# Two fused transformer blocks on one core: modulation sums and filling blocks placed anew in the written-out order

## The reference, cut to what matters

```python
D_MODEL = 1024; SEQ = 256; DEPTH = 4            # two tiles of 128 tokens
def first_block(x, c, ...):
    cond = jax.nn.silu(c)
    for i in range(DEPTH):                      # kinds: gla, sgu, fox, gla
        mod = (cond @ w_mod[i] + b_mod[i])[:, None, :]      # 1024 x 3072 weights per layer
        shift, scale, gate = jnp.split(mod, 3, axis=-1)
        h = rms_norm(x, norm_pre_g[i]) * (1.0 + scale) + shift
        o = (gla_mixer, sgu_mixer, fox_mixer)[i % 3](h, ...)
        x = x + gate * rms_norm(o, norm_post_g[i])
    return x
def second_block(x, ...):
    h = x
    h = h + hybrid_mixer(rms_norm_2(h, norm_mix), ...)      # convolution and dilated attention
    h = h + peer_ffn(rms_norm_2(h, norm_ffn), ...)
    return rms_norm_2(h, final_norm)
def peer_ffn(u, w_query, sub_keys, expert_down, expert_up):
    q = xf @ w_query                            # 8 heads, two halves of 128
    s = einsum(q, sub_keys)                     # 128 scores a half
    ...                                         # top 16 of each half, top 16 of their sums: idx, gates
    a = gelu(einsum('cd,ced->ce', xc, expert_down[ic]))     # 128 rows of 1024 floats a token
    return einsum('ce,ced->cd', gc * a, expert_up[ic])
```

## Time and profile before

| | |
|---|---|
| median of three executions | 1745.24 us (1738.43 to 1745.35) |
| profiled execution, device time | 1739.41 us |
| its span in the trace | 1737.6 us |
| busy: PE, DVE, ACT, POOL | 80%, 60%, 25%, 28% of the span |
| moved by DMA | 591.53 MB, 340 GB/s over the span |
| chain that ended last | DVE 8%, DMA 8%, issue 3%, PE 1% of the span |

### The profile page before, as it was taken

The page is one execution under the profiler, slowest core; times in us unless marked ns, Lnnn a source line. Parts: engine busy times, 40 slices in busy tenths (PEclk is TensorE's granted clock), DMA queues, the critical chain, the costliest instruction groups (busy, mean ns, idle before and its releaser), DMA issues. The chain is left out here.

```text
span 1737.6 us, 13867 instructions
## 1 busy us (share of the span) xinstructions
PE 1393.7 (80%) x4158; PEld 717.6 (41%) x4158; DVE 1047.5 (60%) x2197; ACT 433.1 (25%) x974; POOL 490.7 (28%) x498
## 2 busy tenths in 40 slices
PE   6998988978999999999777777699787647666665
PEld 6454435444444455444354343455333312222222
DVE  3645554553233222313797998788866778877876
ACT  1221413423423421102133232132002221111111
POOL 2101210210000000000445546355344545444441
PEclk9998998989999999999897888798888878898898
DMA  9978884978556776887999989999999999999995
GB/s 386 377 256 303 312 340 171 347 282 295 213 207 219 277 265 242 290 293 265 402 361 357 413 339 403 412 400 413 410 414 414 348 412 422 421 422 421 422 421 248
DMA packets 108941, 591.53 MB, mean 340 GB/s; under 512 B 12450, under 2 KB 12706, under 8 KB 60612
## 3 DMA queue, kind: packets, MB, share of 16 engines
q0 software_dynamic: 67776, 312.56, 45.4%
q1 hardware_dynamic: 41092, 278.10, 42.2%
HBM read 589.55 MB, written 1.05 MB: 340 GB/s over the span
## 5 line engine op out<-in xcount | busy, mean ns | idle before, releaser
L948 PE MATMUL bank<-ring,hT 128*128 128x512 f32 x1888 | 866.6, 615 | 39.6 <-DVE room L1920 12.1
L948 PEld LDWEIGHTS bank<-ring,hT 128*128 128x128 f32 x1888 | 366.5, 198 | 482.2 <-issue 449.8
L877 POOL DMA_INDIRECT room<-in_peer_down,idx x92 | 102.5, 1114 | 525.1 <-DVE idx L1781 401.8
L1798 DVE CUSTOM_DVE_ANT_0 room<-room 128x1024 f32<-128x1024 f32 x180 | 218.6, 1221 | 50.6 <-DMA room<-in_pair,idx 38.4
L1203 PE MATMUL bank<-room 128*128 128x512 f32 x284 | 150.9, 676 | 96.5 <-ACT room L1493 94.2
L1813 DVE SCALAR_TENSOR_TENSOR x<-room,pcoef,x 128x1024 f32<-128x1024 f32 x121 | 155.7, 1287 | 28.0 <-DMA room<-in_peer_up,idx 27.5
L877 POOL DMA_INDIRECT room<-in_peer_up,idx x104 | 114.0, 1096 | 88.6 <-DVE pa L1798 42.3
L1203 PEld LDWEIGHTS bank<-room 128*128 128x128 f32 x284 | 57.5, 215 | 190.8 <-issue 97.2
L849 POOL DMA_DIRECT2D room<-in_w_mod x80 | 42.2, 528 | 326.3 <-DVE room L1567 206.5
L877 POOL DMA_INDIRECT room<-in_pair,idx x88 | 97.0, 1102 | 108.5 <-PE bank L1203 50.6
L927 PE MATMUL bank<-cst,room 128*128 128x128 f32 x424 | 64.7, 297 | 55.3 <-ACT room L1439 24.1
(11 more groups left out here) (304 smaller groups left out, 1527.4 us busy)
## 6 DMA issues: line engine op xcount, KB each, us to landing
ring<-in_wpk SPq DMA_DIRECT2D x248, 1024.0 KB, 7.0
room<-in_w_mod POOLq DMA_DIRECT2D x80, 512.0 KB, 8.2
room<-in_w_mod SPq DMA_DIRECT2D x8, 1024.0 KB, 15.8
room<-in_norm_post_g POOLq DMA_DIRECT2D x4, 512.0 KB, 5.0
rowb<-in_gate_bias SPq DMA_DIRECT2D x4, 512.0 KB, 9.0
room<-in_peer_up,idx POOLq DMA_INDIRECT x104, 12.5
room<-in_peer_down,idx POOLq DMA_INDIRECT x92, 12.4
room<-in_pair,idx POOLq DMA_INDIRECT x88, 14.3
```

The lines of the kernel that those rows point to most:

```text
L877: return pool.indirect_dma_start(out=dst, out_offset=None, in_=A[table][0] if table != "pair" else A[table], in_offset=bass.IndirectOffset ...
L948: last = mm(bank[p][:, :], lhs, ring[:, h % 4, k * N:(k + 1) * N], start=(kk == 0), stop=(h == halves[-1] and k == 3))
L1798: v.tensor_tensor_reduce(out=row, in0=row, in1=u_(g // MINE), scale=1.0, scalar=0.0, op0=ALU.mult, op1=ALU.add, accum_out=pa[:, g // TOPK ...
```

## The change

Six edits, all in what order the same work is issued, but for the first:

1. `PE_PIECES` goes from six pieces to two. Pieces 9, 11, 13 and 15 are summed on DVE, and PE's 32 matmuls for them are gone.
2. A block's pieces are now put behind its `ev` and the steps that follow it, ahead of the next block, instead of straight behind its `mm`. How many a block gets comes from `PIECES_AT`.
3. Gaps: one of the two behind `out2` is moved to between `in2` 3 and `in2` 4 of tile 0.
4. The gap ahead of `merged_T` is gone, so `(1, in2, 0)` comes behind `ho` and `(1, in2, 1)` behind the first ticks.
5. For tile 0 each of the first score steps and `choose` comes one query block sooner.
6. At the end the last four picks make two groups of two, their additions are pulled into ticks 272 to 275, and the last four ticks are gone.

```diff
 def out_chunks(t, L):
-            "gap twice"]
+            "gap" if L == 2 else "gap twice"]
 def fox_chunks(t, L):
             b(3, [], [("unit", t, 1), ("forget_sum", t)]),
+            "gap",
             b(4, [], [("quad_T", t, 0), ("quad_S", t, 0)]),
 def hyb_chunks(t):
             b(0, name="attn"), b(1, name="attn"), b(0, name="conv"), b(1, name="conv"),
-            "gap",
             b(0, name="ho", pre=[("merged_T", t)]), b(1, [("ffn_norm", t)], name="ho"),
             "gap",
-            b(0, name="query", pre=[("norm_in", t, 5)]),
-            b(1, [("score_T", t, 0)], name="query"),
-            b(2, [("score_S", t, 0), ("score_T", t, 1)], name="query"),
+            b(0, [] if t else [("score_T", t, 0)], name="query", pre=[("norm_in", t, 5)]),
+            b(1, [("score_T", t, 0)] if t else [("score_S", t, 0)], name="query"),
+            b(2, ([("score_S", t, 0)] if t else []) + [("score_T", t, 1)], name="query"),
...
-PE_PIECES = (5, 7, 9, 11, 13, 15)
+PE_PIECES = (5, 7)
-TICKS = PICKS + REST + LEAD[1]
+TICKS = PICKS + REST + 2
...
-    return u < 7 * TOPK or u % 4 == 3 or (u % 2 and (u < MINE or u >= PICKS - 8))
+    return u < 7 * TOPK or (u % 4 == 3 and u < PICKS - 4) or (u % 2 and u < MINE) \
+        or u >= PICKS - 2 or (u % 2 and PICKS - 8 <= u < PICKS - 4)
...
 def added_at(v):
+    if v >= PICKS - 8:
+        return tick_of(PICKS - 2) + (v - PICKS + 8) // 2
     return tick_of(v) + LEAD[v // MINE]
...
-GROUPS = [(hh * TOPK, TOPK) for hh in range(PH)] + [(MINE + 4 * m, 4) for m in range(MINE // 4)]
+GROUPS = [(hh * TOPK, TOPK) for hh in range(PH)] + [(MINE + 4 * m, 4) for m in range(MINE // 4 - 1)] \
+    + [(PICKS - 4, 2), (PICKS - 2, 2)]
...
-    if mm[2] == "in0":
-        return (4, 4, 3, 2, 2, 2)[mm[3]]
-    return 4 + mm[3] if mm[2] == "out0" else 3
+PIECES_AT = {"in0": (4, 4, 4, 3, 3, 2), "out0": (4, 2), "in1": (4, 4, 4, 4, 3, 3), "out1": (3, 3),
+             "in2": (3, 3, 3, 3, 2, 2, 2, 2), "out2": (4, 2)}
...
         order += pre
         if mm:
             order.append(mm)
-        for _ in range(pieces_at(mm)):
-            if piece < len(PIECES):
-                order.append(("mod", piece))
-                piece += 1
...
         order += post
         if mm:
+            for _ in range(PIECES_AT[name][n] if name in PIECES_AT else 0):
+                order.append(("mod", piece))
+                piece += 1
             order += pending
             pending = []
-            if name == "query" and n == 2:
+            if name == "query" and n == 1:
                 order.append(("choose", 0))
```

More of the change, by code:

```diff
@@ L272 @@
 DVE_NTH = {u: i for i, u in enumerate(ON_DVE)}
-ADDS = {added_at(v): [v] for v in range(PICKS)}
+ADDS = {k: [v for v in range(PICKS) if added_at(v) == k] for k in range(TICKS)}
 def adds_of(k):
-    return ADDS.get(k, [])
+    return ADDS[k]
 def sums_at(hh):
@@ L289 @@
 EXP_AT = {sums_at(hh): hh for hh in range(T * PH) if hh != PH - 1}
-GROUPS = [(hh * TOPK, TOPK) for hh in range(PH)] + [(MINE + 4 * m, 4) for m in range(MINE // 4)]
+GROUPS = [(hh * TOPK, TOPK) for hh in range(PH)] + [(MINE + 4 * m, 4) for m in range(MINE // 4 - 1)] \
+    + [(PICKS - 4, 2), (PICKS - 2, 2)]
 GROUP_AT = {tick_of(g + n - 1) + 1: i for i, (g, n) in enumerate(GROUPS)}
 def group_of(v):
-    return v // TOPK if v < MINE else PH + (v - MINE) // 4
+    return next(i for i, (g, n) in enumerate(GROUPS) if g <= v < g + n)
 WAY = {"norm_in": 110, "low": 10, "decay": 12, "qk_T": 15, "level": 25, "cross": 30, "heads": 80, "gated_T": 50,
@@ L346, in tick @@
         self.at += 1
-def pieces_at(mm):
-    if mm is None:
-        return 0
-    if mm[2] == "in0":
-        return (4, 4, 3, 2, 2, 2)[mm[3]]
-    return 4 + mm[3] if mm[2] == "out0" else 3
+PIECES_AT = {"in0": (4, 4, 4, 3, 3, 2), "out0": (4, 2), "in1": (4, 4, 4, 4, 3, 3), "out1": (3, 3),
+             "in2": (3, 3, 3, 3, 2, 2, 2, 2), "out2": (4, 2)}
 def make_order():
@@ L397, in make_order @@
                 order.append(("sines", 0))
+            for _ in range(PIECES_AT[name][n] if name in PIECES_AT else 0):
+                order.append(("mod", piece))
+                piece += 1
             order += pending
             pending = []
-            if name == "query" and n == 2:
+            if name == "query" and n == 1:
                 order.append(("choose", 0))
-                rows.tick()
-            if name == "query" and n == 3:
-                rows.tick()
-                rows.tick()
+            if name == "query" and n >= 2:
+                for _ in range(n - 1):
+                    rows.tick()
     order += pending
@@ L992, in _ @@
             pe.wait_ge(S("cond"), 1)
-            for piece in PE_PIECES[:2]:
+            for piece in PE_PIECES:
                 piece_columns(piece, use("mod_cols", 0)[1])
@@ L1002, in _ @@
                         pe.wait_ge(S(f"ev{p}"), n // 2)
-                    if L == 0:
-                        for piece in PE_PIECES[2:]:
-                            piece_columns(piece, p)
                     pe.wait_ge(S(f"sums_init{L % 2}"), sums_set(L))
```

## The result

The changed kernel takes 1753.41 us in the median of 8 runs (1750.9 to 1758.21), the kernel before 1745.3 us (8 runs, 1738.43 to 1752.99). The ratio is 1.0055, with a 95% interval from 1.0039 to 1.0071: slower, by 8 us. The forecast was 1745, no change that can be told (0.48), with 0.30 for slower; the time lies in the range given (1731 to 1759), the direction was not the one forecast. The profiled execution has a span of 1751.3 us, 13.7 longer than the one of before, which was some 6 us under its median.

What follows compares the result with a forecast made beforehand. Before the first gather (821.25 us) PE's work and its waits for DVE bound the kernel, behind it DMA bytes. Terms: -8.5 + 4.5 - 2 + 1.3 = -4.7, so 1739.4 becomes 1744, as a median 1745 us; range 1731 to 1759.

Steps and rivals of the forecast that it cites:

- Start: Up to level 1 of tile 0: +7 us at `low`, of which +3 (between 0 and +7) stays at level 1.
- `out0`: Tile 0's `out0`: shorter wait for `post1` (0.8 us) and 16 matmuls in 7.1 us, +6, account +9.
- `in1`: Up to layer 1's gates: three more pieces on a full DMA, partly regained by +1.5; account from +9 to +6.
- the third rival: DMA-bound already in `in1`: DVE falls behind at both gates, later pieces take 12.4 us to land; 1754 to 1760 us (0.20).
- The second gate: Layer 1's second gate: tile 1's levels 3 and 4 come 13.7 us later, plus 1.9 for the clock; account -9.5.
- the gate's wait is short: Rival: transfers behind layer 1's second gate land in 5.3 us; 1729 to 1735 us (0.22).
- `out1`: Pieces 64 to 66 ahead of tile 1's levels 5 to 7: PE's wait of 3.01 us grows by 3.9; account -13.
- `in2` and the attention: Filling block covers two waits in `in2`, +5 (+2 to +7); fewer late pieces in attention, +3 wait, +2 clock; account -3.
- `out2`: Tile 1's `center` delays DVE's copy for `out2` 0: -5 wait, -2 clock, +1.5 at `post1`, together -5.5; account -8.5.
- First choice, give-back, tail: First gather 12.4 us sooner, 7.9 given back to weight loads (+4.5), -2 for DVE's elementwise work, +1.3 at the end.
- first choice sooner gives nothing: Rival: DVE sets the pace from 885 us on and uses up the 12.4 us; 1750 to 1755 us (0.08).
- two signs of being wrong: DVE's wait behind layer 1's second gate under 5 us, or the first gather before 812 us.

Runs made afterwards that it cites:

- changed_pieces_back: The changed kernel with the modulation pieces back where they stood, in the old counts; all other edits stay: 1737.8 us, 0.996 of the kernel before.
- pieces_moved: The kernel before with only the modulation pieces moved behind evacuations and steps, six pieces still on PE: 1766.2 us, 1.0134.
- two_pieces_on_pe: The kernel before with only two modulation pieces summed on PE, the other pieces where they stood: 1740.69 us, 0.9981.
- levels_first: The changed kernel with the sums of pieces 61 to 63 behind tile 1's levels 3 and 4 on DVE: 1742.76 us, 0.9992 of the kernel before.
- post_row_later: The changed kernel with POOL fetching the next post-norm row behind piece 63, no longer ahead of pieces 61 to 63: 1746.24 us, 1.0017 of the kernel before.
- filler_moved: The kernel before with one filling block moved from behind `out2` to between `in2` 3 and 4: 1747.49 us, 1.0024.
- choice_sooner: The kernel before with no filling block ahead of `merged_T` and the first choice behind query 1: 1736.04 us, 0.9963.
- three_edits_out0: The kernel before with two pieces on PE, first choice sooner, new tail, and `out0`'s pieces behind `post0` and `post1`: 1727.48 us, 0.9908.
- best_combination: The kernel before with two pieces on PE, sooner choice, new tail, `out0`'s pieces behind `post0` and `post1`, post-norm row fetched later: 1720.89 us, 0.9874.

## Why the prediction was wrong

**The step that failed is "Start", "I put +3 there, between 0 and +7".** It measured -2.2. I had seen that the places of pieces 24 to 27 come free some 5 us later, and they did (they were fetched from 65.83 us on, before from 60.01). But I took these 5 us off the +7 won at `low`, as if level 1 came behind `low`. It does not: it waits for the sum of the last piece ahead of it. Piece 27 was summed 6.5 us later than before, one piece fewer stood ahead of level 1 (piece 28 had been summed 4.25 us behind piece 27), and the difference is the -2.2. Of the 6.2 us won at `low` nothing arrives: PE's wait for level 1 grew from 2.49 to 10.88 us. The kernel changed_pieces_back has `low` later and level 1 sooner than the changed kernel. The moved pieces alone (pieces_moved) put the mark at the end of the levels from 118.51 back to 126.81; two_pieces_on_pe, without that, puts it forward to 114.45. The term makes 5.2 of the 9.0 us by which the profiled span (-13.7) missed the sum (-4.7).

**`out0`: right in place, the clock's term wrong.** PE's wait for `post1` fell from 5.00 to 1.00 us. I had taken another 2.2 us for the 16 matmuls behind it, "the longer time is what the lower clock costs", since the engine "had just stood idle". They took 9.33 us with next to no wait ahead of them (9.31 in the earlier trace rows):

```profile
148.62 1.84 PE L1005 MATMUL bank<-ones,gateb 128*128 128x1 f32 x16
150.32 2.53 PE L1005 MATMUL bank<-ones,room 128*128 128x1 f32 x16
153.84 9.33 PE L946 MATMUL bank<-ring,hT 128*128 128x512 f32 x16 [1.00 <-DVE room L1915]
```

The windows of this stretch show the granted clock (last but two): 0.65 from 150 to 155 us, 0.84 from 155 to 165, so part of it at 1.2 GHz and not at 2.4. What stands ahead are 32 matmuls of one column each and 1.00 us of idling. The clock had fallen to 1.2 GHz while PE was still busy with them: granted 0.73 from 151 to 152 us, 0.50 from 152 us on, the last of them ending at 152.85; in the trace of before it is 0.80 from 149 to 150 us, ahead of the wait of 5.00 us. The lower clock stays when the wait goes.

```profile
150.00:155.00 5.00, 4.00 (x23) 3.40 (x23) 2.80 (x11) 0.07 (x1) 0.00 (x0) 0.65 1.02 424
155.00:165.00 10.00, 10.00 (x27) 4.72 (x26) 5.48 (x11) 3.66 (x10) 1.05 (x2) 0.84 0.47 169
```

**`in1`** was -3 and measured -4.3. PE's wait in front of the second gate grew from 5.72 us to 10.01, as the third rival had it, but not to its full price. Part of this comes back in the next row of the account, since PE reaches this mark while DVE still has three pieces to sum between the two gates: before, it waited 1.89 us for them, and now not at all. For that I had put +1.5 into this term.

**The second gate** was right, with its mechanism, its place and the direction: -15.6 forecast, -12.9 measured, and levels_first and post_row_later take it away by either of its two causes. On DVE the levels start 15.1 us later against the evacuation than before (257.64 - 241.94 = 15.70, before 241.78 - 241.18 = 0.60), where 13.7 were forecast. Taken together the two rows are -17.2, forecast -18.6. The rival "the gate's wait is short" (0.22) is excluded. `out1` was right to 0.1 us.

**`in2` and the attention:** +10 forecast, +7.3 measured. Half of it failed: I gave the filling block +5, between +2 and +7, because it covers two waits, and it won 1.1 us, in the changed kernel as in filler_moved. It brings a wait of its own, 5.46 us for ACT's Gelu; I had not asked what the block itself needs. The other half, +5 for the sparser pieces in the attention, measured +5.9. That the filling block alone costs 0.24% is new against the prediction, which had put it near nothing.

**`out2`** was right: 5.15 us of waiting for the copy, as "PE waits near 5 us" had it; -6.9 with the clock, not -5.5, since the +1.5 at `post1` came to +0.75 and the copy behind `out2` waits 1.0 us longer.

**First choice, give-back, tail:** +12.4, -9.9 and +1.3 were forecast, +13.1, -9.1 and +1.4 measured. The rival "first choice sooner gives nothing" is excluded by choice_sooner, though its 1750 to 1755 holds the measured time; that is luck. Neither of the two signs of being wrong came (DVE's wait under 5 us, first gather before 812): the miss lay on the slow side, where I had set none.

The terms that were mis-sized all lay on one side: start 5.2, `out0` 2.2, `in1` 1.3, `in2` 2.7, `out2` 1.4, against 2.7 of the gate and 1.6 of the rest; the last 0.5 of the 9.0 is rounding in the forecast account. With two losses of pieces in the sum (gate and `in1`), the third one, of the same kind and at the start, should have been bounded below nothing.

What stays open: no run gives the start back with the other moved pieces left in place; both attempts made it worse, and only the kernels with the pieces ahead of level 1 as before, place and count, have it. And since two traces of one order can differ by 2 to 5 us at the start, the size of that step (5.2) is worth no more than its confirmation by the means at the end of the levels: 118.3 for three traces of the old order, 121.5 for four of the changed one, so -3.2 where +3 was forecast.

## What to carry to other kernels

Where a short ring of slots feeds a busy DMA, ask of each consumer not what its work costs but when it frees its slot: sums of 1.28 us each, moved behind a few small steps, cost 8 us at the start (pieces_moved), and three of them 11 us behind the gate (levels_first). And add a gain only along the path that the next step waits for: 6 us won at `low` were worth nothing to level 1. A request in an in-order queue that waits for a late event (the row that waits for the gate) is harmless until someone behind it is wanted early; before moving a consumer, read its producer's queue, and mend that queue first: here one number in it took 10.9 us off PE's wait and 7 us off the time. A filling block is not free matter either: it brings its own evacuation, here a table load on ACT ahead of a bank that PE wants.

## What was not expected of the hardware

16 matmuls of 512 columns took 9.31 us behind 5.00 us of idling and 9.33 behind 1.00 us, both behind 32 matmuls of one column; in three_edits_out0 they took 8.83 and in best_combination 10.09 us, again with 1.00 us of wait:

```profile
148.74 10.09 PE L954 MATMUL bank<-ring,hT 128*128 128x512 f32 x16 [1.00 <-DVE room L1923]
```

In this place the lower clock does not go with the wait; the one-column matmuls are what is common to all four.

Pieces of 0.5 MB that the changed kernel issued 1.3 to 1.5 us apart (from 65.83 us on) could be summed only 3.2 to 3.8 us apart; from 70 to 85 us weight halves and pieces share the DMA, whose share is 1.02. There 1.28 us of summing per piece cost nothing, and a slot freed 5 us late does.
